# The first quarter of the modulation matrix in two halves of its columns, and token tiles normalised one by one

## The reference, cut to what matters

```python
mod_x = silu(c) @ w_ada + b_ada            # w_ada is 2048 x 6144, 3 x 2048 columns
sh_x, sc_x, gt_x = split(mod_x, 3)         # shift, scale, gate
mod_c = silu(c_ctx) @ w_ada + b_ada
h_x = rmsnorm(x, g_pre) * (1 + sc_x) + sh_x
h_c = rmsnorm(ctx, g_pre) * (1 + sc_c) + sh_c
p   = h_x @ w_in                           # conv, state-space, Fourier and gate parts
u_c = h_c @ w_in[:, U_OFF:U_OFF + W_SSM]
...
return x + gt_x * rmsnorm(merged @ w_out, g_post)
```

## Time and profile before

| what | value |
|---|---|
| three runs | 2054.59, 2057.17, 2057.46 us; median 2057.17 us |
| the profiled execution | 2054.32 us, span 2052.5 us |
| PE busy | 2008.0 us (98% of the span) |
| DVE busy | 1085.8 us (53%) |
| ACT busy | 594.9 us (29%) |
| loads and stores | 270.72 MB, mean 132 GB/s |

### The profile page before, as it was taken

The page is one execution under the profiler, slowest core; times in us unless marked ns, Lnnn a source line. Parts: engine busy times, 40 slices in busy tenths (PEclk is TensorE's granted clock), DMA queues, the critical chain, the costliest instruction groups (busy, mean ns, idle before and its releaser), DMA issues.

```text
span 2052.5 us, 26821 instructions
## 1 busy us (share of the span) xinstructions
PE 2008.0 (98%) x10086; PEld 1640.1 (80%) x10086; DVE 1085.8 (53%) x1640; ACT 594.9 (29%) x845; POOL 27.4 (1%) x16
## 2 busy tenths in 40 slices
PE   4999999999999999999999999999999999999998
PEld 1568888888888888888888888888888888888886
DVE  4545799999998645554433434332433333333325
ACT  5325343334343322222222222222322222222222
POOL 0003100000000000000000000000000000000000
PEclk9999999999999999999999999999999999999999
DMA  9963544344344544443334444443233333334423
GB/s 361 366 199 116 168 106 109 102 106 108 102 108 112 179 129 133 125 138 108 100 94 138 134 123 138 133 133 104 73 92 102 93 97 97 93 101 154 173 99 128
DMA packets 384079, 270.72 MB, mean 132 GB/s; under 512 B 24820, under 2 KB 349916, under 8 KB 382164
## 3 DMA queue, kind: packets, MB, share of 16 engines
q1 hardware_dynamic: 373728, 265.61, 42.0%
q10 hardware_dynamic: 10292, 4.33, 1.5%
HBM read 251.81 MB, written 18.09 MB: 131 GB/s over the span
## 4 chain that ended last, share of the span: by engine, by line
PE 93%; DVE 3%; ACT 2%; DMA 1%; issue 1%; SPq 0%; ACTq 0%; DVEq 0%
PE ac L753 25%; PE ac L757 25%; PE ac L754 24%; PE ac L938 1%; PE ac L939 1%; PE ac L937 1%; PE ss L815 1%; PE ss L586 1%; PE ss L939 1%; PE ss L938 1%; PE ss L937 1%; PE ac L633 1%; PE ac L634 1%; PE ac L637 1%; DMA wslot<-w_in 1%; PE ss L808 1%
## 5 line engine op out<-in xcount | busy, mean ns | idle before, releaser
L1557 DVE TENSOR_TENSOR wlo<-wslot,whi 128x1024 fp32r<-128x1024 f32 x309 | 378.3, 1224 | 643.4 <-ACT whi L973 639.3
L973 ACT ACTIVATE whi<-wslot 128x1024 fp32r<-128x1024 f32 x327 | 346.9, 1061 | 1244.3 <-PE ac L757 1042.8
L753 PE MATMUL ac<-hxh,whi 128*128 128x512 f32 x1664 | 651.9, 392 | 0.0
L754 PE MATMUL ac<-hxl,whi 128*128 128x512 f32 x1664 | 647.8, 389 | 0.0
L757 PE MATMUL ac<-hxh,wlo 128*128 128x512 f32 x1664 | 411.2, 389 | 0.9 <-DVE wlo L1557 0.9
L753 PEld LDWEIGHTS ac<-hxh,whi 128*128 128x128 f32 x1664 | 312.4, 188 | 67.4 <-issue 2.9
L757 PEld LDWEIGHTS ac<-hxh,wlo 128*128 128x128 f32 x1664 | 312.3, 188 | 66.1 <-DVE wlo L1557 1.3
L754 PEld LDWEIGHTS ac<-hxl,whi 128*128 128x128 f32 x1664 | 312.4, 188 | 63.8
L753 PE MATMUL ac<-bah,whi 128*128 128x512 f32 x384 | 149.4, 389 | 0.0
L754 PE MATMUL ac<-bal,whi 128*128 128x512 f32 x384 | 149.4, 389 | 0.0
L757 PE MATMUL ac<-bah,wlo 128*128 128x512 f32 x384 | 94.8, 389 | 0.0
(11 more groups left out here) (359 smaller groups left out, 2076.0 us busy)
## 6 DMA issues: line engine op xcount, KB each, us to landing
wslot<-w_in SPq DMA_DIRECT2D x224, 512.0 KB, 3.8
ring<-w_ada SPq DMA_DIRECT2D x64, 512.0 KB, 8.4
gwt<-w_ada SPq DMA_DIRECT2D x128, 128.0 KB, 2.5
wslot<-w_out SPq DMA_DIRECT2D x32, 512.0 KB, 3.6
wslot<-proj_a SPq DMA_DIRECT2D x16, 512.0 KB, 4.1
wslot<-proj_b SPq DMA_DIRECT2D x16, 512.0 KB, 4.1
wslot<-proj_c SPq DMA_DIRECT2D x16, 512.0 KB, 3.9
xn<-x SPq DMA_DIRECT2D x4, 1024.0 KB, 9.6
```

The costliest lines, as they stand in the source:

```text
L753: mm(ac[:, bank, :], w, xh, start=(v == 0 and q == 0), stop=False)
L754: mm(ac[:, bank, :], w, xl, start=False, stop=False)
L973: cp = lambda o, i, scale=1.0: nc.scalar.activation(o, i, ACT.Copy, scale=scale)
L1557: tt(wlo[:, s, :], wslot[:, s, :], whi[:, (U0[k] + j) % 2, :].bitcast(F32), ALU.subtract)\
```

## The change

The first eight units of w_ada are cut otherwise. Units 0 to 3 now hold the first 256 columns of the quarter (shift and scale) for all 2048 rows, units 4 to 7 the other 256; a unit is still 1 MB, in rows of 256 numbers (1 KB) in place of 512 (2 KB). The row of each half lies in a PSUM bank of its own, and `cols`, `columns` and the copy of the row are done in halves, so that `x_piece(0, 0)` and `x_piece(0, 1)` depend on units 0 to 3 only. The four token tiles are normalised one by one, and the polynomials on DVE are placed between the four calls of `token_scale`. `early_turn(t)` now transposes twelve blocks of one token tile, in three groups of four, into a ring of five PSUM banks (`ac` 0 to 3 and `ss` 0); group n (counted over all tokens) waits for the copy of group n - 5. The order of the loads changes a little (both context tiles ahead of unit 8).

```diff
 # SP
             if n >= 4:
                 sp.wait_ge(ada_used, n - 3)
+            if n < 8:
+                half, r = n // 4, n % 4
+                for h in range(2):
+                    sp.dma_start(halves(n)[:, :, h, :],
+                                 w_ada[r * 512:(r + 1) * 512, h * D + half * 256:h * D + (half + 1) * 256]
...
-            if n % 8 >= 6:
+            if n in (3, 7):
+                first_unit(n // 4)
+            if n == 7:
+                for t in range(CT):
+                    sp.dma_start(cn[:, t, :], ctx[0, t * 128:(t + 1) * 128, :]).then_inc(c_in, 16)
+            if n > 8 and n % 8 >= 6:
                 first_unit(n // 8 * 2 + n % 2)
 # PE
-        def early_turn(k):
-            pe.wait_ge(y_done, TT)
-            if k >= 4:
-                pe.wait_ge(xp_done, k - 3)
+        def early_turn(t):
+            pe.wait_ge(y_done, t + 1)
+            for g in range(PARTS):
+                n = t * PARTS + g
+                if n >= 5:
+                    pe.wait_ge(xp_done, n - 4)
+                for k in range(4):
+                    c0 = (4 * g + k) * 128
+                    last = tr(early_bank(n)[:, k * 128:(k + 1) * 128], xn[:, t, c0:c0 + 128], ident[:, :])
+                last.then_inc(xp_ps, 1)
...
+        for n in range(4):
+            if n < 2:
+                early_turn(n)
             ada(n)
...
+            if n == 2:
+                early_turn(2)
...
+        early_turn(3)
+        cols(0, range(2))
+        ada(4)
+        ada(5)
+        pe.wait_ge(xp_done, TT * PARTS)
+        x_piece(0, 0, range(4))
+        ada(6)
+        ada(7)
+        x_piece(0, 1, range(4))
+        cols(0, range(2, 4))
         ada(8)
         ada(9)
+        x_piece(0, 2, range(4))
+        ada(10)
+        x_piece(0, 3, range(4))
...
 # ACT
+        def early_out(t):
+            for g in range(EARLY // 4):
+                n = t * (EARLY // 4) + g
+                act.wait_ge(xp_ps, n + 1)
...
+        token_square(0)
+        token_root(0)
+        token_square(1)
+        token_norm(0)
+        token_root(1)
+        token_square(2)
+        token_norm(1)
+        token_root(2)
+        token_square(3)
+        token_norm(2)
+        token_root(3)
+        early_out(0)
+        token_norm(3)
+        early_out(1)
+        rows_half(0)
+        early_out(2)
+        early_out(3)
...
 # DVE
+        token_scale(0, 1, 1)
+        exp(a7[:, 0:1], ldt[:, :], a1[:, 0:1], a2[:, 0:1], a3[:, 0:1], a4[:, 0:1], ei[:, 0:1])
+        token_scale(1, 1, 2)
+        link(ts_(a0, lre, a7[:, 0:1], None, ALU.mult))
+        exp(a6, a0, a1, a2, a3, a4, ei[:, :])
+        token_scale(2, 1, 3)
+        sines()
+        token_scale(3, 1, 4)
+        cosines()
```

More of the change, by code:

```diff
@@ L580, in ada @@
             if r == 0 and q:
-                pe.wait_ge(col_rd, q)
+                pe.wait_ge(col_rd, q + 1)
             pe.wait_ge(ada_in[n % 4], 32 * (n // 4 + 1))
+            if n < 8:
+                r = n % 4
+                for kk in range(4):
+                    for h in range(2):
+                        p = 64 * (kk % 2) + 32 * h
+                        last = mm(ss[p:p + 2, 2 + n // 4, 0:256], cs[:, 4 * r + kk, :], halves(n)[:, kk, h, :],
+                                  start=(r == 0 and kk < 2), stop=(r == 3 and kk > 1))
+                last.then_inc(ada_used, 1)
+                return
             for kk in range(2):
@@ L588, in ada, with cols @@
             last.then_inc(ada_used, 1)
-        def cols(q):
-            pe.wait_ge(row_cp, q + 1)
-            for k in range(4):
+        def cols(q, ks=range(4)):
+            if q or ks[0]:
+                pe.wait_ge(col_rd, q + 1 if q else 1)
+            pe.wait_ge(row_cp, q + 2 if q else ks[0] // 2 + 1)
+            for k in ks:
                 last = mm(ss[:, 2, 4 * k:4 * k + 4], rows[:, k * 128:(k + 1) * 128],
@@ L680, in p0_c @@
             last.then_inc(p0_ps, 1)
-        for n in range(8):
+        for n in range(4):
+            if n < 2:
+                early_turn(n)
             ada(n)
[L684 to L691, removed]
+            if n == 2:
+                early_turn(2)
+        pe.wait_ge(vec_in, 64)
+        tr(ss[:, 1, 0:V_END], vrow[:, :], ident[0:V_END, 0:V_END])
+        tr(ss[:, 1, 128:128 + G], drow[:, :, :].rearrange("n l h -> n (l h)"), ident[0:G, 0:G]).then_inc(vec_ps, 1)
+        early_turn(3)
[8 more added lines that the diff above has]
+        cols(0, range(2, 4))
         ada(8)
         ada(9)
[L694 to L697, removed]
+        x_piece(0, 2, range(4))
+        ada(10)
+        x_piece(0, 3, range(4))
         turn(0, 4)
-        ada(14)
[L700 to L711, removed]
+        ada(11)
+        turn(0, 5)
+        ada(12)
+        c_piece(0, 0)
+        ada(13)
+        ada(14)
+        c_piece(0, 1)
+        ada(15)
+        c_piece(0, 2)
+        cols(1)
+        c_piece(0, 3)
+        for n in range(16, 20):
+            ada(n)
+        for q in range(1, 3):
+            x_piece(q, 0, range(4))
+            ada(8 * q + 12)
+            x_piece(q, 1, range(4))
+            turn(q, 4)
+            ada(8 * q + 13)
+            x_piece(q, 2, range(4))
+            ada(8 * q + 14)
+            turn(q, 5)
+            x_piece(q, 3, range(4))
             ada(8 * q + 15)
@@ L989, in rows_cp, with rows_half @@
             cp(rows[:, :], ss[:, 2, :]).then_inc(row_cp, 1)
+        def rows_half(half):
+            act.wait_ge(ada_used, 4 * half + 4)
+            cp(rows[:, half * 256:(half + 1) * 256], ss[:, 2 + half, 0:256]).then_inc(row_cp, 1)
         def high(q, n):
@@ L1472, in _ @@
         for q in range(4):
+            columns(q, range(2 if q == 0 else 4))
+            modulate(q, 0)
             if q == 0:
                 lo_first(0)
-            columns(q)
-            modulate(q, 0)
             low(q, 0)
@@ L1479, in _ @@
             low(q, 1)
-            if q:
+            if q == 0:
+                zoh()
+                columns(0, range(2, 4))
+            else:
                 lo_first(2 * q)
             modulate(q, 2)
+            if q == 0:
+                lo_first(1)
             low(q, 2)
```

138 lines of the change are left out of this document (72 added, 66 removed).

## The result

The changed kernel takes 2063.03 us (median of 8 runs, 2061.83 to 2065.09), the kernel before 2057.28 us (8 runs, 2053.77 to 2059.25). The ratio is 1.0033, with a 95% interval of 1.0024 to 1.0043: slower by 0.33%, or 6.8 us (4.9 to 8.8). The ratio is not the quotient of the two medians: these lie 5.7 us apart. The profiled execution took 2062.8 us with a span of 2061.0 us, 8.5 us above the profiled execution of before, whose 2054.32 us lay near the lowest of the kernel's runs.

A forecast was written before the change was run, and what follows sets the result against it. The load stream, emptied by PE's wait for the fifth bank, was taken to bound the opening: +5.1 us at `x_piece(1, 0)` plus 0.7 for the clock, +5.8, giving 2060.1 profiled and 2063.0 as median; range 2057 to 2067.

The forecast's parts named there:

- The chain over DVE: Opening: exponentials and sine put token 3's root at 31.5 to 32.0, first `xT` copy at 32.6, `ada(1)` done at 35.5.
- The queue runs dry: Load queue, opening: empty some time between 30 and 33 us, until late unit 5 flows again from 37.1.
- The price of 1 KB runs: Loads of units 5 to 7: 1 KB runs cost 8% more time, +0.65 us (bounds 0 and 2.0).
- Unit 9 at 60.3: Load stream: unit 9, ending 7.87 MB after the restart at 37.1, counts as landed at 60.3.
- Unit 18 at 87.4, unit 19 at 90.1: Load stream: landing times after 19.40 MB at 387 GB/s; PE waits ahead of `ada(18)` and `ada(19)`.
- `x_piece(0, 0)` at 46.8: PE, opening: this piece starts near 46.8, 4.5 us early, since it no longer needs the whole quarter.
- `x_piece(1, 0)` at 91.5: PE: this piece starts after `ada(19)` at 91.5, against 86.43 in the kernel before, +5.1 us.
- The clock: PE at `x_piece(1, 0)`: waits ahead of `ada(18)` and `ada(19)` lower the clock; half of 1.43 taken, +0.7 us.
- From there to the end a constant distance: PE, from `x_piece(1, 0)` near 91.5 to the end: the distance to the kernel before stays constant.
- the stream makes up most of it: Rival, opening: earlier restart, earlier landing and no slow clock leave +2.4 us, 2059.6; chance 0.18.
- The queue never runs dry: Rival, opening: unit 5 issued before the queue empties, unit 19 at 84.1, -1.3 us, 2055.9; chance 0.05.
- PE's gain whole: Rival, opening: all of PE's freed time comes through, -7.5 us, 2049.7; chance 0.03.

The follow-up runs named there:

- before, with the wait: Kernel before plus one line: PE waits for all four normalised tokens ahead of the second unit's product; 2061.46 us, ratio 1.0036.
- All three: Changed kernel with units 0 to 3 before later tokens' transposes, context transposes and DVE polynomials later, context loads in their old places; 2054.41 us, ratio 0.9994.
- context later alone: Changed kernel with only the context transposes and pieces one or two units later on PE, bank wait left in; 2061.2 us, ratio 1.0025.
- units first: Changed kernel with the products of units 0 to 3 ahead of the transposes of tokens 1 to 3 on PE; 2057.33 us, ratio 1.0009.
- units first, context later: Changed kernel with units 0 to 3 ahead of later tokens' transposes and context transposes one or two units later on PE; 2055.19 us, ratio 0.9995.
- polynomials later: Changed kernel with the four token scales first on DVE, sines, cosines and powers behind the first products, PE order kept; 2057.78 us, ratio 1.0010.
- six banks: Changed kernel with a sixth PSUM bank in the early transposes' ring, so the stop moves behind `ada(1)` and `ada(2)`; 2058.17 us, ratio 1.0011.
- before, context early: Kernel before with both context tiles loaded ahead of unit 8, nothing else changed; 2056.94 us, ratio 1.0011.

## Why the prediction was right, step by step

- **The chain over DVE** gave the root of token 3 at 31.5 to 32.0; it started at 31.24. The first copy was to end at 32.6, and PE went on at 31.98. "A third of 2.82" for the four transposes measured 1.12, at the low clock. `ada(1)` was to be done at 35.5; it is half of the 3.59 from 33.02, so 34.8. "1.89 at the slow clock" is read from the duration alone: the table of the kernel before has a granted clock of 1.00 there, though the product is as long as at 49.54, so its early clock is no guide.

```profile
30.00:35.00 5.00, 4.00 (x20) 2.71 (x21) 3.30 (x16) 3.17 (x4) 0.00 (x0) 1.00 1.05 387
```

- **The queue runs dry** between 30 and 33: at 31.5. "Flow again from 37.1": 36.4, reckoned as if it began at the full rate (203 GB/s from 36 to 37 are 0.6 us of 348). The 0.7 us come from `ada(1)`; from its end I took 1.6 us, and 1.6 were measured here. In "before, with the wait" the same reckoning gives 2.0 (from 33.3; 0.66 MB from 34 to 37 are 1.7 us of 387).
- **The price of 1 KB runs**, worked out as 8%: from 20 to 30 us, with a full queue, the changed kernel moved 3.53 MB, 353 GB/s against 386 for 2 KB runs, 9% more time, with some longer runs among them. "All three" has nothing but 1 KB runs from 30 to 40 us and moved 3.46 MB, 346 GB/s, 12% more time:

```profile
q1 hardware_dynamic: 3478, 3.46, 109.0%
```

  The Trainium skill (DMA: Bandwidth & Descriptors, Specifications) has line rate from 512 B up; these two stretches speak against it at 1 KB. The price was 0.65 us of the sum, and of small weight: the versions that keep 1 KB runs and lose the hole are within about 0.1% of the kernel before. No run has the 1 KB runs alone.
- **Unit 9 at 60.3**: 60.27. This exact hit is luck: it hides two errors against each other, the earlier restart and a unit that counted as landed later, when 18.99 MB had moved, 1.16 MB past its own sum (4.19 of tokens, ten units, two `first_unit`, the context: 17.83) and not 0.87: -0.7 and +0.75 us.
- **Unit 18 at 87.4, unit 19 at 90.1**: 88.18 and 90.87. Here a step was incomplete. "From there the stream decides" took the queue as full up to unit 19. From 68 to 76 it was not: 1.7 us of stream. The chain shows SP waiting for PE there; that PE was late because of units 8 and 9 and the low clock behind them is my reading, and no run tests it. Against that, unit 19 landed when 30.02 MB had moved, only 0.66 past its sum of 29.36, where unit 9 had been 1.16 past its own: 1.3 us back. Two more dips, at 66 and 76, make most of the rest of the +0.8. In "context later alone" part of the dips is gone.
- **`x_piece(0, 0)` at 46.8**: 45.34, 1.5 us sooner. Nothing of the sum hung on it.
- **`x_piece(1, 0)` at 91.5**, +5.1: it measured 92.69, +6.3. I gave `ada(19)` 1.4 us, and it took the slow 1.82.
- **The clock**, half of 1.43: 0.85 in `x_piece(1, 0)`. So the sum of +5.8 was +7.1 at 96.49 by the same rows.
- **"From there to the end a constant distance"** fails by the low clock at 153 to 156, 1.4 us more. That "PE never catches up" holds: at the end the distance is still 8.5 us.

By the profiled executions the change is worth +8.5 us where I summed +5.8, all of the difference on the slow side; it sits in the ring, in the clock at 90 and in the clock at 153. By the medians it is 5.7, by the ratio 6.8 us with bounds 4.9 and 8.8. The mechanism and the place were right, and the size is about 1 us short by the ratio. That the median lands within 0.1 us of the predicted 2063.0 is luck: the measures of one and the same change differ by up to 2.8 us, and the terms were off by as much. The range of 2057 to 2067 was a weak test besides, since its lower end is the time of the kernel before.

Of the rivals, "the stream makes up most of it" is out, since landing and clock both went against it. "The queue never runs dry" did not happen here, but as a kernel of its own it gave 2055.19 us, 1.0 us under the kernel before by the ratio, where it had 2055.9 and 1.3. "PE's gain whole" did not come in any kernel here: with the stops removed unit 19 still lands at 83.98. "The clock stays low longer" has some truth: one fall at 153 and not the whole price.

What the experiments show about the cause: the stop alone, in the kernel before, gives a loss as large as that of the whole change (1.0036); the order on PE alone, in the changed kernel, takes 4.9 us of it back; a sixth bank, which keeps the stop and moves it two units, takes 4.5 back; a shorter chain on DVE, which ends the stop at 24 instead of 32, takes 4.7 back with PE's order untouched. The order of the context loads alone is worth 0.1%, at the edge of what was measured. Three of these kernels stay 0.1% above the kernel before; what of that is the 1 KB runs, the order or the clock is open. How the loss splits between hole, dips and clock is read from one profile and not from runs.

## What to carry to other kernels

A wait on an in-order engine is priced by what stands behind it when it ends, and not by its length alone: here the loads that PE frees behind a wait of 9 us cost some 6 us, and a wait of 5 us that ended at the same time, with two units less behind it, left a loss of 2. Where a small ring feeds an engine, look up the last instruction that frees a place and make sure that no wait for another engine stands ahead of it; two more units used before the stop were enough.
In a stretch that the stream bounds, work made ready earlier buys nothing unless the last load of the stretch also lands earlier. Read the load rate in 1 us steps there, since a hole in it can lie under a busy PE, as at 32 to 36.

## What the hardware showed that was not expected

**The clock falls at like waits in one kernel and not in another.** The waits near 145 and 150 us are nearly the same in both kernels: ahead of the later one PE stood 2.13 us in the changed kernel and 2.12 in the one before. Yet the changed kernel has the low clock at 153 to 156, while the same table of the kernel before, with all its work 7 us earlier, shows none from 144 on:

```profile
144.00:147.00 3.00, 2.63 (x13) 2.19 (x14) 1.27 (x3) 0.00 (x0) 0.00 (x0) 1.00 0.00 0
147.00:150.00 3.00, 3.00 (x17) 2.48 (x16) 1.49 (x4) 0.63 (x1) 0.00 (x0) 1.00 0.02 5
150.00:153.00 3.00, 3.00 (x15) 2.47 (x14) 0.92 (x2) 2.21 (x4) 0.00 (x0) 1.00 0.00 0
```

The profiles of "units first", "units first, context later", "polynomials later", "all three" and "context later alone" have such a fall between 141 and 156; those of "six banks", "before, with the wait" and "before, context early" don't. What decides it is open. It is worth about 1.5 us, as much as many edits; whether it is part of why the runs of one kernel spread over 5 us was not measured.

**A restart of an empty queue** took 1.2 to 1.4 us in two kernels, from the end of the product that freed the ring's place to the first data: 34.8 to 36.0 in the changed kernel, 33.3 to between 34.5 and 34.75 in "before, with the wait".

**Runs of 1 KB** cost 9 to 12% at a full queue: 346 to 354 GB/s in the kernels with half units, against 386 in 2 KB runs.
